# Moving the last step of a strip's recurrence from ahead of the next strip's last weight tile to behind the next strip's convolution, in a hybrid decoder layer

## Chip, cores and metric

One Trainium2 chip, one core. The metric is the device time of one launch in microseconds (us), lower is better; several runs of a kernel are compared by their median.

## What is computed

One inference step of one decoder layer, for 256 prompt tokens and 8 x 8 sample tokens together (320 tokens), model width 2048. The input projection feeds three token mixers (RG-LRU, gated DeltaNet, causal pooling); their gated outputs are summed, projected and added to the residual; a squared-ReLU MLP follows. The part that matters here is the RG-LRU, cut from the reference:

```python
xl, gl, q, k, v, z, b_raw, a_raw, u_pool, g_lru, g_dn, g_pool = split_cols(xn @ w_in)
xl, new_lru_buf = causal_dwconv(xl, lru_buf, lru_conv_w, lru_conv_b)      # 4 taps over time
h, h_last = rg_lru(xl, w_a, b_a, w_x, b_x, lam, h0)
# r, i = sigmoid(xl @ w_a + b_a), sigmoid(xl @ w_x + b_x);  a = exp(-8 r softplus(-lam))
# h[t] = a[t] h[t-1] + sqrt(1 - a[t]^2) (i[t] xl[t])
o_lru = (h * jax.nn.gelu(gl)).astype(x.dtype)
merged = sigmoid(g_lru) * (o_lru @ w_br_lru) + ...
```

## The kernel before

Channels lie on partitions, the 320 tokens on columns. Every weight passes through the kernel once, in tiles of 512 x 256 values (128 x 1024 on chip), through a ring of four slots. SyncE starts the load of a tile into `raw`. ScalarE rounds it to `hi` (`split` in its program, L617), VectorE forms `lo = raw - hi` (`split`, L885), and TensorE multiplies hi and lo parts with the activations' hi and lo parts: 24 matmuls of 320 columns for a tile (`tile`, L1436 to L1438). The four steps are tied by counts:

- SyncE may load tile n+4 when `lo` of tile n is written (`lo_ready`).
- ScalarE may write `hi` of tile n+4 when TensorE is done with tile n (`tile_used`).
- TensorE starts tile n when its `lo` is there, and writes into a PSUM bank when VectorE has emptied it (`evacuated`).

The RG-LRU's 1024 channels are worked on in four strips of 256. A strip has eight weight tiles, 0 to 3 for `xl` and 4 to 7 for `gl`. Strip 0 is written out ahead of a loop; the loop (`Fori(1, 4)`) runs strips 1 to 3 on TensorE, ScalarE and VectorE alike. When `xl` is done, VectorE convolves it in time (`lru_conv`: L885 empties two banks, then L888 and L892, 4 + 12 instructions, into `scratch`), which sets `conv_ready`. TensorE's `gates` waits for it after tile 7 and runs four small products (L1539). Then the next strip's tile 0 begins.

The recurrence of strip `it-1` is worked off during strip `it`, in six steps that stand between the tiles' splits. `walk` (VectorE) places a step with position p behind the split of tile p-1. `walk_ahead` (ScalarE) places it behind the split of tile p, one further on. The order is the same program order as written, engine by engine; nothing reorders it. The steps, by position:

- 3, step 0: the gates' tanh (ScalarE L701, L703), the log of a (VectorE).
- 4, step 1: exp, tanh, square (ScalarE L708 to L710), one VectorE product.
- 5, steps 2 and 3: root (ScalarE L713), the scan (VectorE L1110), and the emptying of the two banks of `gl`.
- 6, step 4: the inner part of GELU (VectorE), its tanh (ScalarE L719).
- 7, step 5: two products on VectorE (L892) form the output; ScalarE rounds it to `o_hi` (L722); VectorE subtracts to `o_lo` (L885) and counts `o_ready`.
- 8: on VectorE `lru_conv` of the strip itself.

Step 5 has a hand-over in both directions: ScalarE waits for `of_ready`, set by VectorE's second product, and VectorE waits for `ohi_ready`, set by ScalarE. Of the four `o_hi`/`o_lo` strips TensorE reads nothing before the next stage (`gated`, L1640 on), whose tile 5 waits for `o_ready` of all four.

The last strip's recurrence (strip 3) is worked off in the first iteration of that next stage, `gated(0, GPL_N, ...)`, with the same positions 3 to 7.

The functions `lru_steps`, `walk`, `walk_ahead`, `lru`, `lru_step`, `conv` and `gates` are those that the text below follows.

Of the kernel before, what the change touches and what calls it, by code (L numbers as in the profile page):

```python
# [46 lines left out]
LRU_N, LRU_T = QKV_N + 6 * 8, QKV_T + 6 * 4  # L47
# [35 lines left out]
def cols(t, index, width, lo=0, n=None, rows=P):  # L83

    n = width if n is None else n
    if isinstance(index, int):
        return t[0:rows, index * width + lo:index * width + lo + n]
    return t[0:rows, bass.ds(index * width + lo, n)]


def build(nc, A):
    with ExitStack() as ctx:
# [455 lines left out]
        def joined(a, b):  # L548

            return {i: [*a.get(i, ()), *b.get(i, ())] for i in {*a, *b}}  # L550

        def walk(split, n0, per, it, tiles, after):

            for j in range(tiles):
                split(n0, per, it, j)
                for step in after.get(j + 1, ()):
                    step()

        def walk_ahead(split, n0, per, it, tiles, after):

            split(n0, per, it, 0)
            for j in range(tiles):
                if j + 1 < tiles:
                    split(n0, per, it, j + 1)
                for step in after.get(j + 1, ()):
                    step()

        def lru_steps(step, it):

            return {pos: [lambda k=k: step(it, k) for k in ks]  # L570
                    for pos, ks in ((3, (0,)), (4, (1,)), (5, (2, 3)), (6, (4,)), (7, (5,)))}

        def qkv_steps(rms, silu, rows):

# [32 lines left out]
        def _(act):  # L607
# [117 lines left out]
            def lru(it, after):  # L725
                walk_ahead(split, LRU_N, 8, it, 8, after)
# [3 lines left out]
                    6: [lambda: row_scalars(3)], 7: [lambda: root(2)]})  # L730
            with act.Fori(1, 4) as it:
                ch.enter(it, 1, LINKS["rglru"])
                lru(it, lru_steps(lru_step, it - 1))
                ch.leave(3, "rglru")

            def gate(it, s, t0, g0):
# [38 lines left out]
            def late(it, t0, h0):  # L775

                steps = {2: [lambda: gate(it, 1, t0, 0)]}
                return steps if h0 is None else joined(steps, dn_steps(dn_step, it + h0, False, True))

            gated(0, GPL_N, GPL_T, 0, lru_steps(lru_step, 3), True)  # L780
            with act.Fori(1, 4) as it:
                gated(it, GPL_N, GPL_T, 0, late(it - 1, GPL_T, 0))
# [95 lines left out]
        def _(dve):  # L878
# [76 lines left out]
            def conv(n0, per, it, j, t, tval, strip, first, ct, bias):  # L955

                tile_done(n0, per, it, j)
                if not first:
                    dve.wait_ge(tail_copied, strip)
                sv = [PAD[m][:, NP + 3:347].rearrange("p (b t) -> p b t", b=DB) for m in range(2)]  # L960
                for m in range(2):
                    scaled(t + m, PAD[m][:, 3:3 + NP], sv[m][:, :, CW - 1:CW - 1 + DT])
                dve.wait_ge(evacuated, tval)
                dve.wait_ge(prefix_ready, strip + 1)
                for w in range(CW):
                    for m in range(2):
                        k = cols(PRM, ct, CW, C_CW + m * CW + w, 1)
                        for src, dst in ((PAD[m][:, w:w + NP], CV[:, m * N:m * N + NP]),
                                         (sv[m][:, :, w:w + DT],
                                          CV[:, m * N + NP:(m + 1) * N].rearrange("p (b t) -> p b t", b=DB))):  # L970
                            if w:
                                ins = stt(dst, src, k, dst, ALU.mult, ALU.add)
                            elif bias is None:
                                ins = ts(dst, src, k, ALU.mult)
                            else:
                                ins = ts(dst, src, k, ALU.mult, bias[m], ALU.add)
                    if w < CW - 1:
                        link(ins)
                ins.then_inc(conv_ready, 1)
# [96 lines left out]
            def lru_conv(it):  # L1076
                conv(LRU_N, 8, it, 3, 0, it * 4 + (LRU_T + 2 + RING), it + 12, False, it * 2 + 24,
                     [cols(PRM, it, 2, C_CB + m, 1) for m in range(2)])
# [47 lines left out]
                    tt(cols(OL, it, 2 * N), GL, cols(OH, it, 2 * N).bitcast(F32), ALU.subtract).then_inc(o_ready, 1)  # L1126

            def lru(it, after):
                walk(split, LRU_N, 8, it, 8, {**after, 8: [lambda: lru_conv(it)]})

            lru(0, {4: [lambda: silu(11)], 6: [lambda: row_scalars(3)], 7: [row_norms]})
            with dve.Fori(1, 4) as it:
                ch.enter(it, 1, LINKS["lru"])
                lru(it, lru_steps(lru_step, it - 1))
                ch.leave(3, "lru")

            def gate(n0, t0, it, s):
# [664 lines left out]
```

## Time and profile before

| | |
|---|---|
| time, median of 3 runs | 2188.42 us (2185.13 to 2188.83) |
| the profiled execution: its own time | 2186.87 us |
| its span, first to last instruction | 2185.1 us |
| TensorE busy | 2149.7 us (98%) |
| VectorE busy | 1222.3 us (56%) |
| ScalarE busy | 784.2 us (36%) |
| GpSimd busy | 175.9 us (8%) |
| mean DMA traffic | 141 GB/s |
| mean granted TensorE clock | 0.994 |
| chain of work that ended last, by engine | TensorE 84%, VectorE 9%, ScalarE 3%, issue 3%, DMA 1% |

The page gives each engine's busy time as a share of the span. TensorE (PE) is busy nearly all the time by its records; the matmuls are pipelined and their ends modelled, so that their starts, not their durations, give the pace. The granted clock is 1.00 at full speed (2.4 GHz) and 0.50 at half (1.2 GHz). The loop over RG-LRU strips 1 to 3 lies between 229 and 325 us of the span.

### The profile page before, as it was taken

The numbers are of one execution on the slowest core, as the hardware profiler recorded it, in microseconds if no ns is written. First come the engines' busy times: TensorE is split into PE (matmuls) and PEld (weight loads), VectorE is DVE, ScalarE is ACT, GpSimd is POOL, SyncE is SP. The second block draws the span as 40 slices with busy tenths as digits, with TensorE's granted clock in tenths as the row PEclk, the third lists the DMA queues.
The fourth block names the chain that finished last, engine by engine and source line by source line (L and its number), as shares of the span: only waits on it lengthen the run. The fifth ranks groups of instructions, "written<-read, shape, count | busy, mean of one in ns | idle before, by whom it ended". The sixth has DMA issues, their size and how long they took to land.

```text
span 2185.1 us, 35787 instructions
## 1 busy us (share of the span) xinstructions
PE 2149.7 (98%) x14515; PEld 2094.4 (96%) x14515; DVE 1222.3 (56%) x1996; ACT 784.2 (36%) x946; POOL 175.9 (8%) x340
## 2 busy tenths in 40 slices
PE   9999998999999999999999999999999999999997
PEld 9998997999998999999999999999999999999997
DVE  7996785555566655555454554444444444444444
ACT  6434553222232222333334343333333333333343
POOL 7000012110022110010000000000000000000001
PEclk9999999999999999999999999999999999999998
DMA  6544443343353433336544444444444444444443
GB/s 218 163 143 128 140 129 121 116 119 116 116 165 106 118 117 116 116 107 212 150 148 155 145 144 152 147 153 146 154 145 154 146 154 146 154 145 154 147 144 106
DMA packets 295609, 308.96 MB, mean 141 GB/s; under 512 B 9712, under 2 KB 290416, under 8 KB 295232
## 3 DMA queue, kind: packets, MB, share of 16 engines
q1 hardware_dynamic: 291616, 291.54, 43.1%
q0 software_dynamic: 3584, 15.55, 2.4%
q8 instruction: 90, 1.47, 0.3%
q14 instruction: 31, 0.25, 0.0%
q10 hardware_dynamic: 288, 0.15, 0.0%
HBM read 298.83 MB, written 8.37 MB: 141 GB/s over the span
## 4 chain that ended last, share of the span: by engine, by line
PE 84%; DVE 9%; ACT 3%; issue 3%; DMA 1%; DVEq 0%; ACTq 0%; SPq 0%
PE main L1436 26%; PE main L1438 25%; PE main L1437 25%; PE aux L1556 6%; DVE scratch L892 2%; DVE lo L885 2%; DVE scratch L885 2%; ACT hi L617 1%; DMA raw<-in_w_in 1%; DVE scratch L889 1%; PE aux L1539 0%; PE aux L1529 0%; DVE scratch L888 0%; DVE merged L885 0%; PE aux L1660 0%
## 5 line engine op out<-in xcount | busy, mean ns | idle before, releaser
L885 DVE TENSOR_TENSOR lo<-raw,hi 128x1024 fp32r<-128x1024 f32 x546 | 667.2, 1230 | 566.6 <-ACT hi L617 560.0
L617 ACT ACTIVATE hi<-raw 128x1024 fp32r<-128x1024 f32 x546 | 573.3, 1056 | 920.6 <-PE main L1438 904.8
L1436 PE MATMUL main<-x_hi,hi 128*128 128x320 f32 x2688 | 842.8, 314 | 2.5 <-DVE x_lo L892 2.0
L1438 PE MATMUL main<-x_hi,lo 128*128 128x320 f32 x2688 | 831.5, 309 | 0.0
L1437 PE MATMUL main<-x_lo,hi 128*128 128x320 f32 x2688 | 831.5, 309 | 0.0
L1436 PEld LDWEIGHTS main<-x_hi,hi 128*128 128x128 f32 x2688 | 505.7, 188 | 10.6 <-issue 5.0
L1437 PEld LDWEIGHTS main<-x_lo,hi 128*128 128x128 f32 x2688 | 505.8, 188 | 0.7
L1438 PEld LDWEIGHTS main<-x_hi,lo 128*128 128x128 f32 x2688 | 505.4, 188 | 0.0
L1436 PE MATMUL main<-o_hi,hi 128*128 128x320 f32 x1408 | 444.6, 316 | 4.6 <-DVE o_lo L885 4.6
L1438 PE MATMUL main<-o_hi,lo 128*128 128x320 f32 x1408 | 435.6, 309 | 0.0
L1437 PE MATMUL main<-o_lo,hi 128*128 128x320 f32 x1408 | 435.5, 309 | 0.0
L1436 PEld LDWEIGHTS main<-o_hi,hi 128*128 128x128 f32 x1408 | 264.8, 188 | 9.2 <-issue 7.1
L1437 PEld LDWEIGHTS main<-o_lo,hi 128*128 128x128 f32 x1408 | 265.0, 188 | 2.0 <-issue 1.9
L1438 PEld LDWEIGHTS main<-o_hi,lo 128*128 128x128 f32 x1408 | 264.9, 188 | 0.0
L1556 PE MATMUL aux<-scratch 128*128 128x128 f32 (+5 forms) x1056 | 155.9, 284 | 6.2 <-DVE scratch L1200 3.2
L1556 PEld LDWEIGHTS aux<-scratch 128*128 128x128 f32 (+1 forms) x1056 | 130.4, 185 | 26.2 <-DVE scratch L885 10.2
L885 DVE TENSOR_TENSOR qkv<-main,qkv 128x320 f32<-128x320 f32 (+1 forms) x144 | 64.0, 486 | 72.9 <-PE main L1438 72.8
L1436 PE MATMUL main<-merged_hi,hi 128*128 128x320 f32 x256 | 79.1, 309 | 0.0
L1437 PE MATMUL main<-merged_lo,hi 128*128 128x320 f32 x256 | 79.1, 309 | 0.0
L1438 PE MATMUL main<-merged_hi,lo 128*128 128x320 f32 x256 | 79.1, 309 | 0.0
L885 DVE TENSOR_TENSOR scratch<-scratch,aux 128x256 f32<-128x256 f32 (+2 forms) x144 | 45.2, 359 | 51.7 <-PE aux L1556 43.6
L544 POOL COPY qkv<-gate 128x640 f32<-128x640 f32 x1 | 0.7, 724 | 867.7 <-ACT gate L854 867.7
(253 smaller groups left out, 1190.8 us busy)
## 6 DMA issues: line engine op xcount, KB each, us to landing
raw<-in_w_in SPq DMA_DIRECT2D x210, 512.0 KB, 3.8
raw<-in_w_up SPq DMA_DIRECT2D x128, 512.0 KB, 3.8
raw<-in_w_down SPq DMA_DIRECT2D x128, 512.0 KB, 3.4
raw<-in_w_back SPq DMA_DIRECT2D x80, 512.0 KB, 3.4
scratch<-in_s_in POOLq DMA_DIRECT2D x8, 512.0 KB, 4.7
out_s_out<-scratch POOLq DMA_DIRECT2D x8, 512.0 KB, 4.6
merged<-in_x SPq DMA_DIRECT2D x8, 320.0 KB, 7.8
qkv<-in_x POOLq DMA_DIRECT2D x1, 2560.0 KB, 10.2
```

The lines of the kernel that those rows point to most:

```text
L544: pool.tensor_copy(acc, GS[:]).then_inc(sq2_used, 1)
L617: act.activation(HI[:, slot * TILE:(slot + 1) * TILE], RAW[:, slot * TILE:(slot + 1) * TILE], ACT.Copy).then_inc(hi_ready, 1)
L885: return dve.tensor_tensor(out, a, b, op)
L889: dve.tensor_scalar(out, a, s1, None, op0)
L892: return dve.scalar_tensor_tensor(out=out, in0=a, scalar=s, in1=b, op0=op0, op1=op1)
L1436: pe.matmul(bank, hi, xh, start=first, stop=False)
L1437: pe.matmul(bank, hi, xl, start=False, stop=False)
L1438: return pe.matmul(bank, lo, xh, start=False, stop=last)
L1556: return pe.matmul(out, a, b, start=True, stop=True)
```

## The change

On VectorE, inside the loop, step 5 of the strip before goes from position 7 to position 8, and `joined` puts it behind the convolution there: the order split 6, step 5, split 7, convolution becomes split 6, split 7, convolution, step 5. On ScalarE the same `last=8` names another position, but `walk_ahead` has no split between positions 7 and 8: its order stays split 7, step 5, next strip's split 0. The steps of strip 3, in the stage after the loop, keep position 7.

```diff
-        def lru_steps(step, it):
+        def lru_steps(step, it, last=7):
 
             return {pos: [lambda k=k: step(it, k) for k in ks]
-                    for pos, ks in ((3, (0,)), (4, (1,)), (5, (2, 3)), (6, (4,)), (7, (5,)))}
+                    for pos, ks in ((3, (0,)), (4, (1,)), (5, (2, 3)), (6, (4,)), (last, (5,)))}
...
             with act.Fori(1, 4) as it:
                 ch.enter(it, 1, LINKS["rglru"])
-                lru(it, lru_steps(lru_step, it - 1))
+                lru(it, lru_steps(lru_step, it - 1, 8))
...
             def lru(it, after):
-                walk(split, LRU_N, 8, it, 8, {**after, 8: [lambda: lru_conv(it)]})
+                walk(split, LRU_N, 8, it, 8, joined({8: [lambda: lru_conv(it)]}, after))
...
             with dve.Fori(1, 4) as it:
                 ch.enter(it, 1, LINKS["lru"])
-                lru(it, lru_steps(lru_step, it - 1))
+                lru(it, lru_steps(lru_step, it - 1, 8))
```

## Rows read from the trace of the kernel before

**Rows 1.** Waits of TensorE between 225 and 425 us: total, times, longest.
```profile
PE main L1436 <- DVE o_lo L885: 4.6, 1, 4.6
PE aux L1539 <- DVE scratch L892: 4.0, 3, 1.3
```

**Rows 2.** Timeline of TensorE around the gates: start, duration, instruction [idle before].
```profile
260.71 0.55 PE L1436 MATMUL main<-x_hi,hi 128*128 128x320 f32 x1
...
288.96 0.31 PE L1438 MATMUL main<-x_hi,lo 128*128 128x320 f32 x1
290.58 2.42 PE L1539 MATMUL aux<-scratch 128*128 128x320 f32 x8 [1.31 <-DVE scratch L892]
292.59 0.55 PE L1436 MATMUL main<-x_hi,hi 128*128 128x320 f32 x1
```

**Rows 3.** Timeline of VectorE, strip 2 of the loop, end.
```profile
277.62 1.22 DVE L885 TENSOR_TENSOR lo<-raw,hi 128x1024 fp32r<-128x1024 f32 x1
279.07 1.68 DVE L892 SCALAR_TENSOR_TENSOR scratch<-scratch 128x640 f32<-128x640 f32 x2 [0.23 <-ACT scratch L719]
281.78 0.83 DVE L885 TENSOR_TENSOR o_lo<-scratch,o_hi 128x640 f32 x1 [1.03 <-ACT o_hi L722]
282.52 1.22 DVE L885 TENSOR_TENSOR lo<-raw,hi 128x1024 fp32r<-128x1024 f32 x1
283.66 1.01 DVE L885 TENSOR_TENSOR scratch<-main,rms_scale 128x256 f32<-128x256 f32 x4
...
286.42 4.11 DVE L892 SCALAR_TENSOR_TENSOR scratch<-scratch,params 128x256 f32<-128x256 f32 x12 [0.16 <-DVE scratch L888]
290.44 3.49 DVE L885 TENSOR_TENSOR lo<-raw,hi 128x1024 fp32r<-128x1024 f32 x3
```

**Rows 4.** Timeline of ScalarE, strip 2 of the loop; the last two rows: strip 3.
```profile
264.66 1.06 ACT L617 ACTIVATE hi<-raw 128x1024 fp32r<-128x1024 f32 x1 [1.60 <-PE main L1438]
...
268.18 1.06 ACT L617 ACTIVATE hi<-raw 128x1024 fp32r<-128x1024 f32 x1 [0.44 <-PE main L1438]
...
278.94 1.05 ACT L617 ACTIVATE hi<-raw 128x1024 fp32r<-128x1024 f32 x1
280.88 0.74 ACT L722 ACTIVATE o_hi<-scratch 128x640 f32 x1 [0.89 <-DVE scratch L892]
281.64 1.28 ACT L617 ACT_TABLE_LOAD   x1
282.93 2.01 ACT L617 ACTIVATE hi<-raw 128x1024 fp32r<-128x1024 f32 x2
...
312.76 0.74 ACT L722 ACTIVATE o_hi<-scratch 128x640 f32 x1 [0.89 <-DVE scratch L892]
313.41 2.00 ACT L617 ACTIVATE hi<-raw 128x1024 fp32r<-128x1024 f32 x2
```

**Rows 5.** Timeline of ScalarE: first step of strip 3's recurrence, behind the loop.
```profile
324.93 0.53 ACT L701 ACTIVATE scratch<-aux,params 128x320 f32<-128x320 f32 x1 [6.14 <-PE aux L1539]
```

**Rows 6.** SyncE's load started after the next strip's first `lo`: time to landing.
```profile
L242 SPq DMA_DIRECT2D raw<-in_w_in x1: 373/373/373, 259.9 to 259.9; - x1
DMA to landing us min/median/max: 3.7/3.7/3.7
...
DMA to landing us min/median/max: 4.8/4.8/4.8
```

**Rows 7.** Timeline of TensorE: starts after waits of four lengths.
```profile
9.04 0.39 PE L1436 MATMUL main<-x_hi,hi 128*128 128x320 f32 x1 [1.99 <-DVE x_lo L892]
...
347.08 0.61 PE L1436 MATMUL main<-o_hi,hi 128*128 128x320 f32 x1 [4.59 <-DVE o_lo L885]
347.48 0.47 PE L1437 MATMUL main<-o_lo,hi 128*128 128x320 f32 x1
347.75 0.47 PE L1438 MATMUL main<-o_hi,lo 128*128 128x320 f32 x1
...
359.93 0.44 PE L1582 MATMUL aux<-ident,scratch 128*128 128x128 f32 x2 [2.14 <-DVE scratch L885]
...
685.65 0.69 PE L1582 MATMUL aux<-ident,scratch 128*128 128x128 f32 x2 [2.86 <-DVE scratch L885]
```

**Rows 8.** Windows: length, busy by engine (PE, PEld, DVE, ACT, POOL), PEclk, DMA share, GB/s.
```profile
5.00:10.00 5.00, 3.01 (x23) 2.85 (x23) 3.15 (x8) 3.96 (x7) 4.27 (x26) 1.00 1.07 376
10.00:20.00 10.00, 10.00 (x71) 10.00 (x70) 6.09 (x8) 6.55 (x11) 8.06 (x8) 1.00 1.06 373
255.00:265.00 10.00, 8.67 (x53) 7.77 (x52) 8.52 (x19) 3.18 (x6) 0.00 (x0) 1.00 0.39 111
360.00:364.00 4.00, 4.00 (x17) 3.42 (x18) 0.72 (x3) 0.78 (x3) 0.00 (x0) 0.57 0.02 4
684.80:691.70 6.90, 6.05 (x23) 5.26 (x24) 1.85 (x8) 1.47 (x4) 0.00 (x0) 0.51 0.00 0
```

## Prediction

> **What bounds the kernel now.** I read three views in this order. First the busy shares: TensorE 98%, so only its idle time and its clock can move the end. Then the waits of TensorE in the stretch of the change [rows 1]: three waits of 1.3 us at the gates (L1539), each released by the convolution on VectorE, and one of 4.6 us at tile 5 of the next stage, released by `o_lo` of strip 3. Then the timelines of the three engines over one strip, to see what leads to the convolution's end.
>
> I take strip 2 of the loop as the template and count from the start of its tile 0 on TensorE, 260.71; call that T. The next strip's tile 0 starts at 292.59, T+31.88 [rows 2]. Eight tiles end for issue at T+28.40 (last matmul starts at 288.96, and they follow each other by 0.15), TensorE waits until 290.58, and the gates take 2.01 to the next tile 0. The floor of a strip is thus 28.40 + 2.01 = 30.41, and 1.47 of the 31.88 is the wait (1.31 by the records, whose ends are modelled).
>
> What ends that wait is a loop through all engines. ScalarE's `hi` of tile 4 starts at 264.66, T+3.95, released by TensorE's end of tile 0; `hi` of tile 5 at T+7.47, released by the end of tile 1; `hi` of tile 7 at T+18.23 [rows 4]. VectorE then does step 5 at 279.07, waits 1.03 for `o_hi`, writes `o_lo`, does `lo` of tile 7 at 282.52 and the convolution up to 290.53 [rows 3]. The gates start 0.05 later.
>
> **The change, part by part.** No instruction is added or removed; the same 3 + 1 instructions of step 5 run three times in another place. No DMA is issued by step 5. ScalarE's instruction stream is the same as before. GpSimd isn't passed: its tail copies wait for the two banks emptied by the convolution, which come earlier, and its prefixes for the next convolution are copied long before.
>
> (a) What is taken from ahead of the convolution. `lo` of tile 7 no longer waits for step 5, only for `hi` of tile 7, which ends at 278.94 + 1.05 = 279.99 [rows 4]. It starts at 280.03, T+19.32, in place of 282.52: 2.49 earlier. From there to the convolution's end are 8.01 (282.52 to 290.53) [rows 3], so it ends at T+27.33. TensorE comes to the gates at T+28.40. The wait of 1.47 is gone, with 1.07 to spare. The gates are done at T+30.41.
>
> (b) What is put behind it. VectorE's two products take 1.68 from T+27.25 to T+28.93. ScalarE has stood at step 5 since `hi` of tile 7 ended (T+19.28), as it can't pass its own wait. `o_hi` starts 0.13 after the products (280.75 to 280.88), at T+29.06. **Queued behind that wait on ScalarE are the next strip's `hi` 0 and 1**, which before were done at about T+24.2. At the loop's start stands an activation table load, then `hi` 0: 2.05 after the start of `o_hi` (280.88 to 282.93) [rows 4]. So `hi` 0 runs from T+31.11 to T+32.15. VectorE needs 0.04 and 1.22 for `lo` 0: T+33.41. TensorE starts tile 0 at about T+33.46, not at T+30.41. That is 33.46 - 31.88 = **1.58 later than before**, in place of 1.47 earlier: the wait has moved from before the gates to after them, and grown to 3.05. `o_lo`, 0.83 on VectorE, fits in while ScalarE does its table load and `hi` 0.
>
> (c) How often. Three iterations have the moved step. The first two are followed by the loop's start with its table load: 2 x 1.58 = 3.16. The third is followed by the next stage, where `hi` 0 comes 0.65 after the start of `o_hi` (312.76 to 313.41) [rows 4]: T+29.71. Tile 0 would start at T+32.0 to 32.1, 0.2 late. That stage has a wait of 4.6 at tile 5, but it absorbs nothing, for what ends it is strip 3's recurrence, which starts on ScalarE with L701 at 324.93, T+32.34 in its strip (tile 0 at 292.59) [rows 5]. Ahead of L701 stand `hi` 0, 1, 2. Before, they were done early and L701 waited for the gates. Now they run from T+29.71 at about 1.0 each (2.00 for two), so that L701 starts at T+32.6: 0.25 late, and tile 5 with it. Sum so far: 3.16 + 0.25 = **3.4 us slower**.
>
> (d) The next strip's own loop. `hi` 4 there waits for TensorE's tile 0 (T'+3.95, T' the late start) and for its load, started at 259.94, 0.23 after `lo` 0 ended at 259.71 [rows 6]. With a landing time of 3.7 it is there at T'+3.9 and costs nothing; with 4.8, as once in this trace, `hi` 4 starts at T'+5.0, and 0.44 of that is caught by the wait ahead of `hi` 5 [rows 4], so 0.6 is lost. Bounds: 0 and 0.6 per strip; I take 0, as two of three loads landed in 3.7. The two banks of `gl` are emptied in the same relation to T' as before.
>
> (e) The clock. The wait after the gates isn't harmless in its length. By the records the gates end 0.40 after the next tile could start (290.58 + 2.42 = 293.00 against 292.59), so the idle time of TensorE is 33.46 - 30.41 - 0.40 = 2.65. In this trace waits of 1.31 (255 to 265 us) and of 1.99 (at 9.04) left the granted clock at 1.00, that of 2.14 at 359.93 was followed by half clock (0.57 over 360 to 364), that of 2.86 at 685.65 by 0.51 over 6.9 us, and that of 4.59 by half clock as well [rows 7, 8]. The new wait of 2.65 lies between two that were followed by half clock, not far above one that wasn't. At half clock matmuls start every 0.27 (347.48, 347.75) in place of 0.147, so 3.4 us of it cost 3.4 x (1 - 0.147/0.27) = 1.5. It falls on tiles 0 and 1, whose ends release `hi` 4 and 5, so it delays the whole loop of (a) and (b). Bounds for one such wait: 0 (as after 1.99) and 3.1 (6.9 us at half clock). There are two such waits. I give each 6 in 10 to bring the clock down, and take one of the two: **1.5**. The third wait (T+30.81 to T+32.05, about 1.2) is like those before the gates that did nothing.
>
> The Trainium skill, "TensorE: Matmul & The Clock Gate", section "Why this matters for your kernels", advises only against longer idle gaps between bursts than this one; by it the clock would stay up here and the sum would be 3.4. The waits of 2.14 and 2.86 in this trace speak against it. I keep it as a rival.
>
> The table load costs 1.28 and `hi` 0 starts directly behind it, 2.05 after `o_hi` began [rows 4]. The Trainium skill, "ScalarE: Activation LUTs", section "What ACT_TABLE_LOAD costs", adds a drain of about 1.38 to each switch of tables; by it two loads on the path would cost about 2.8 more, a sum of 7.7 as an estimate from the page. The row shows no such gap between `o_hi` (ends 281.62), the load and `hi` 0, so I go by the row.
>
> **Sum.** 3.16 + 0.25 + 1.5 = 4.9. The span becomes 2185.1 + 4.9 = 2190.0, the profiled execution's own time 2186.87 + 4.9 = 2191.8. That execution lies 1.55 below the median of the runs; on the median I predict 2188.42 + 4.9 = **2193.3 us**. The runs shown spread over 3.7 us, so I call under 0.2% (4.4 us) no difference.
>
> **The rivals.**
>
> *No fall of the clock* (0.17). Only the moved wait counts: +3.4, 2191.8. For it: the wait of 1.99 left the clock alone. Against: those of 2.14 and 2.86 didn't.
>
> *Both waits bring it down* (0.28): +6.4, 2194.8; if one of the stretches is as long as the one at 685 us, +8.0.
>
> *Faster: the hold on ScalarE is hidden* (0.05). If `hi` 0 of the next strip were worked off before ScalarE stands at `of_ready`, the three waits at the gates would go and nothing come back: -1.47 x 3 = -4.4, 2184.0. It decides at tile 0's `lo`: ready before T+30.41 it is a gain, and my chain has it at T+33.41. For it speaks that ScalarE is idle for 9.8 us while it stands there and the slots are free; against it the program order, in which step 5 comes first.
>
> *The table load costs more when nothing hides it* (0.05): if VectorE's `lo` 0 finds `hi` 0 later than 2.05 after `o_hi` by another 1.4, twice, the sum is 7.7, 2196.1. Against it stands the row of the same load behind the same `o_hi`.
>
> **How the numbers follow.** My forecast, one fall, gets 0.42; the rest, 0.03, is for what I don't see. The low end: no fall, 2191.8, less some 2 for the runs' spread and for the half-clock stretches elsewhere, which may come out shorter: 2189.5. The high end: two falls with a longer stretch, 2196.4, and a late load in each strip, 1.2: 2197.5. Faster: the hidden hold and a little for the spread, 0.07. The case without a fall lies mostly within 0.2%, the forecast is 0.22% and so about 4 in 10 within, two falls hardly: 0.31 for the same. Slower: 0.62.
>
> **What the profile after would show.** Right: no wait of L1539 for L892; two new waits of about 3 us of L1436 (tile 0) for `lo` L885, and one near 1.2; `o_hi` (L722) about 8 us later in the strip, after an idle time of about 9.8 on ScalarE; strips 33.5 us or more apart, and half clock for some us after at least one of the new waits; the wait of 4.6 at tile 5 unchanged. Wrong: `hi` 0 of the next strip ahead of `o_hi`, or the convolution still ending after TensorE's tile 7, or a wait at tile 5 that shrinks by what came before it.

## The result

| | before | changed |
|---|---|---|
| median of 20 runs | 2186.55 us (2182.57 to 2188.83) | 2192.27 us (2190.01 to 2194.83) |
| ratio to before | | 1.0028, 95% interval 1.0022 to 1.0035 |
| profiled execution: span | 2185.1 us | 2193.1 us |
| mean granted clock there | 0.994 | 0.992 |

The changed kernel is slower by 5.7 us on the medians, by 4.8 to 7.7 us on the interval. I had forecast 4.9 more, 2193.3 us against a median before of 2188.42 from three runs; with twenty runs that median is 1.9 lower. So the time itself is only 1.0 off because two misses cancel in part: the base was 1.9 too high and the added time 0.8 too low. The profiled execution of the changed kernel is the slowest of its twenty runs (2194.83), so its trace shows more than the median's loss: 8.0 in place of 5.7.

The two largest groups of TensorE's waits between 225 and 425 us of the changed kernel (who waited, for whom, total, times, longest), to be read against [rows 1]:

```profile
PE main L1436 <- DVE lo L885: 6.9, 3, 2.8
PE main L1436 <- DVE o_lo L885: 4.8, 1, 4.8
```

The three waits of L1539 for the convolution are gone. In their place L1436, tile 0 of the next strip, waits three times for its `lo`. The timeline of TensorE shows where, against [rows 2]: the gates of strips 1, 2 and 3 start at once, and tile 0 behind them is late.

```profile
257.31 2.31 PE L1539 MATMUL aux<-scratch 128*128 128x320 f32 x8
262.44 0.63 PE L1436 MATMUL main<-x_hi,hi 128*128 128x320 f32 x1 [2.82 <-DVE lo L885]
262.87 0.47 PE L1437 MATMUL main<-x_lo,hi 128*128 128x320 f32 x1
263.13 0.47 PE L1438 MATMUL main<-x_hi,lo 128*128 128x320 f32 x1
...
293.46 2.31 PE L1539 MATMUL aux<-scratch 128*128 128x320 f32 x8
298.57 0.41 PE L1436 MATMUL main<-x_hi,hi 128*128 128x320 f32 x1 [2.80 <-DVE lo L885]
...
328.37 2.31 PE L1539 MATMUL aux<-scratch 128*128 128x320 f32 x8
331.99 0.41 PE L1436 MATMUL main<-x_hi,hi 128*128 128x320 f32 x1 [1.31 <-DVE lo L885]
...
354.61 0.60 PE L1436 MATMUL main<-o_hi,hi 128*128 128x320 f32 x1 [4.76 <-DVE o_lo L885]
```

ScalarE's timeline over strip 2's end, against [rows 4]: 9.74 us of idle time in front of `o_hi`, then the table load, then four `hi` in one go.

```profile
283.29 1.04 ACT L617 ACTIVATE hi<-raw 128x1024 fp32r<-128x1024 f32 x1
294.08 0.74 ACT L722 ACTIVATE o_hi<-scratch 128x640 f32 x1 [9.74 <-DVE scratch L892]
294.83 1.28 ACT L617 ACT_TABLE_LOAD   x1
296.13 3.90 ACT L617 ACTIVATE hi<-raw 128x1024 fp32r<-128x1024 f32 x4
```

And VectorE's, against [rows 3]: the last tile's `lo` waits for its `hi`, the convolution follows (L892, x12, up to 292.37), then the two products; the next strip's `lo` waits for ScalarE.

```profile
284.37 1.23 DVE L885 TENSOR_TENSOR lo<-raw,hi 128x1024 fp32r<-128x1024 f32 x1 [1.17 <-ACT hi L617]
...
288.26 4.11 DVE L892 SCALAR_TENSOR_TENSOR scratch<-scratch,params 128x256 f32<-128x256 f32 x12 [0.15 <-DVE scratch L888]
292.28 1.68 DVE L892 SCALAR_TENSOR_TENSOR scratch<-scratch 128x640 f32<-128x640 f32 x2
294.98 0.82 DVE L885 TENSOR_TENSOR o_lo<-scratch,o_hi 128x640 f32 x1 [1.03 <-ACT o_hi L722]
297.22 3.50 DVE L885 TENSOR_TENSOR lo<-raw,hi 128x1024 fp32r<-128x1024 f32 x3 [1.41 <-ACT hi L617]
```

The windows around the end of the first new wait and behind the second (length, busy time by engine, granted clock, DMA) show the clock, against [rows 8]:

```profile
261.00:268.00 7.00, 5.56 (x21) 5.57 (x22) 5.77 (x7) 4.55 (x8) 0.00 (x0) 0.55 0.62 180
...
299.00:303.00 4.00, 4.00 (x19) 4.00 (x19) 2.85 (x5) 2.69 (x6) 0.00 (x0) 0.57 0.74 198
```

Tile 5 of the next stage starts at 354.61, before at 347.08 [rows 7]: 7.5 of the 8.0 by which this profiled execution is longer are there before the stage's tile 5.

### The profile page after: what moved, and what is told of

The parts are those of the page before. It is cut to its first block, busy times and chain, and to the rows that moved or that the text cites. A ratio compares the mean times of both kernels' runs of the same rounds, so it can differ in the third digit from the quotient of the medians.

```text
span 2193.1 us, 35787 instructions
## 1 busy us (share of the span) xinstructions
PE 2154.9 (98%) x14515; PEld 2099.5 (96%) x14515; DVE 1221.5 (56%) x1996; ACT 783.3 (36%) x946; POOL 174.9 (8%) x340
## 4 chain that ended last, share of the span: by engine, by line
PE 84%; DVE 9%; ACT 3%; issue 3%; DMA 1%; DVEq 0%; ACTq 0%; SPq 0%
PE main L1436 26%; PE main L1438 25%; PE main L1437 25%; PE aux L1556 6%; DVE scratch L892 2%; DVE lo L885 2%; DVE scratch L885 2%; ACT hi L617 2%; DMA raw<-in_w_in 1%; DVE scratch L889 1%; PE aux L1529 0%; DVE merged L885 0%; DVE scratch L888 0%; PE aux L1660 0%; DVE qkv L892 0%
## 5 line engine op out<-in xcount | busy, mean ns | idle before, releaser
L1436 PE MATMUL main<-x_hi,hi 128*128 128x320 f32 x2688 | 844.2, 314 | 9.2 <-DVE lo L885 7.4
L1436 PEld LDWEIGHTS main<-x_hi,hi 128*128 128x128 f32 x2688 | 507.3, 189 | 18.5 <-issue 11.7
L1436 PE MATMUL main<-o_hi,hi 128*128 128x320 f32 x1408 | 445.3, 316 | 4.8 <-DVE o_lo L885 4.8
L1436 PEld LDWEIGHTS main<-o_hi,hi 128*128 128x128 f32 x1408 | 265.4, 188 | 9.5 <-issue 7.4
L1436 PE MATMUL main<-merged_hi,hi 128*128 128x320 f32 x256 | 79.1, 309 | 0.0
L885 DVE TENSOR_TENSOR o_lo<-scratch,o_hi 128x640 fp32r<-128x640 f32 (+1 forms) x44 | 36.3, 825 | 60.7 <-ACT o_hi L845 50.4
```

The lines of the kernel that those rows point to most:

```text
L885: return dve.tensor_tensor(out, a, b, op)
L1436: pe.matmul(bank, hi, xh, start=first, stop=False)
```

## The experiments

Each of the eight kernels was timed beside the kernel before. The table gives the ratio with its 95% interval, and what it is in us of 2187. The last column is the distance from one strip's gates to the next strip's in the profiled execution (from the first L1539 of one to the first of the other), strips 0 to 1, 1 to 2, 2 to 3: the pace of the loop, of which eight tiles and the gates alone take 30.4.

| kernel | median, us | ratio (95%) | in us | gates to gates, us |
|---|---|---|---|---|
| before | | 1 | | 31.81, 31.89, 31.89 |
| change | 2192.27 | 1.0028 (1.0022 to 1.0035) | +6.1 | 30.32, 36.15, 34.91 |
| e1 products ahead, `o_lo` behind | 2182.24 | 0.9978 (0.9969 to 0.9987) | -4.8 | 30.32, 30.31, 30.30 |
| e2 e1 with ScalarE's hold | 2187.94 | 1.0002 (0.9993 to 1.0011) | +0.4 | 30.32, 32.46, 33.99 |
| e3 change, wait filled | 2190.27 | 1.0016 (1.0007 to 1.0025) | +3.5 | 30.31, 33.41, 33.40 |
| e4 change, ScalarE's loop written out | 2186.90 | 1.0001 (0.9992 to 1.0010) | +0.2 | 30.38, 31.96, 31.92 |
| e5 before, ScalarE's loop written out | 2185.23 | 0.9999 (0.9990 to 1.0008) | -0.2 | 31.77, 31.87, 31.86 |
| e6 step 5 between split and convolution | 2192.77 | 1.0032 (1.0021 to 1.0044) | +7.0 | 32.76, 32.82, 34.43 |
| e7 e1 and strip 3's tail closed up | 2178.47 | 0.9967 (0.9955 to 0.9979) | -7.2 | 30.32, 30.32, 30.30 |
| e8 e6, wait filled | 2188.89 | 1.0011 (1.0002 to 1.0020) | +2.4 | 32.75, 32.84, 32.83 |

**e1: only the wait for `o_hi` and the subtraction go behind the convolution.** Step 5 on VectorE is cut in two: the two products, which release ScalarE, stay where they were before the change. The last strip's step 5, in the stage behind the loop, keeps its order. The edit is against the kernel before.

```diff
-                else:
+                elif k == 5:
                     dve.wait_ge(gth_ready, it + 1)
                     link(stt(GL, G2, 1.0, GL, ALU.add, ALU.mult))
                     dve.wait_ge(h_ready, it + 1)
                     stt(GL, TR, 0.5, GL, ALU.mult, ALU.mult).then_inc(of_ready, 1)
+                else:
                     dve.wait_ge(ohi_ready, it + 1)
...
-                walk(split, LRU_N, 8, it, 8, {**after, 8: [lambda: lru_conv(it)]})
+                walk(split, LRU_N, 8, it, 8, joined({8: [lambda: lru_conv(it)]}, after))
...
-                lru(it, lru_steps(lru_step, it - 1))
+                lru(it, joined(lru_steps(lru_step, it - 1), {8: [lambda: lru_step(it - 1, 6)]}))
```

> Only the last of step 5's instructions, the subtraction to o_lo with its wait for o_hi, goes behind the convolution; the two products stay ahead of the last tile's split, so ScalarE is released as early as before. My theory (the loss comes from ScalarE standing in front of the next strip's first tile): the convolution still starts 1.8 us earlier, ends 0.4 us ahead of TensorE's tile 7, and hi of tile 0 is not held, so the three waits of 1.47 us go and nothing comes back: 4.4 us faster than before. Rival one (it is the wait for o_hi and the o_lo subtraction behind the convolution that make the next lo late): slower by about 1 us a strip. Rival two (the convolution does not set the strip's pace): no change.

It is 4.8 us faster than before. The timelines of ScalarE, VectorE and TensorE over strip 2's end (line numbers have moved by one on TensorE):

```profile
279.15 0.74 ACT L722 ACTIVATE o_hi<-scratch 128x640 f32 x1 [0.89 <-DVE scratch L892]
279.91 1.28 ACT L617 ACT_TABLE_LOAD   x1
281.20 2.01 ACT L617 ACTIVATE hi<-raw 128x1024 fp32r<-128x1024 f32 x2
```
```profile
277.35 1.68 DVE L892 SCALAR_TENSOR_TENSOR scratch<-scratch 128x640 f32<-128x640 f32 x2 [0.23 <-ACT scratch L719]
278.95 1.22 DVE L885 TENSOR_TENSOR lo<-raw,hi 128x1024 fp32r<-128x1024 f32 x1
...
282.82 4.11 DVE L892 SCALAR_TENSOR_TENSOR scratch<-scratch,params 128x256 f32<-128x256 f32 x12 [0.15 <-DVE scratch L888]
286.85 0.82 DVE L885 TENSOR_TENSOR o_lo<-scratch,o_hi 128x640 f32 x1
287.58 3.49 DVE L885 TENSOR_TENSOR lo<-raw,hi 128x1024 fp32r<-128x1024 f32 x3
```
```profile
287.38 2.32 PE L1540 MATMUL aux<-scratch 128*128 128x320 f32 x8
289.29 0.55 PE L1437 MATMUL main<-x_hi,hi 128*128 128x320 f32 x1
```

VectorE loses neither the 1.03 in front of `o_lo` nor a wait for `hi` 7, the convolution is done at 286.93, 0.45 before TensorE wants it, and ScalarE has the next strip's `hi` 0 and 1 done by 283.2. No wait of TensorE is left in the loop, and ScalarE isn't held at step 5 in front of the next strip's tiles. Both rivals fall: the `o_lo` subtraction behind the convolution costs nothing, and the convolution did set the pace.

**e2: the hold alone is put back.** ScalarE is made to stand at step 5 until the convolution is done; VectorE's order stays e1's.

```diff
                     act.wait_ge(of_ready, it + 1)
+                    if not isinstance(it, int):
+                        act.wait_ge(conv_ready, it + 14)
```

> The kernel of e1, in which ScalarE alone is made to wait for the end of the convolution before it rounds to o_hi; VectorE's order is e1's. My theory: hi 0 of the next strip comes 2.05 us after o_hi, which starts at T+28.1, tile 0 starts at T+32.5 in place of T+31.88: 0.6 us a strip slower than before in the first two, strip 3's recurrence about 0.6 us earlier than before behind the third; in sum 0.6 us slower than before and 5 us slower than e1, idle time of TensorE at tile 0 about 1.7 us, clock not touched. Rival (the place of VectorE's work, not ScalarE's hold, makes the loss): as e1, 4.4 us faster.

It is level with before (+0.4), 5.2 us slower than e1, as expected. The profile adds what the expectation had wrong: the third distance is 33.99. TensorE's second new wait, of 1.86, was followed by half clock, shown here by its timeline and the window behind it (line numbers moved by two and three):

```profile
293.53 0.41 PE L1439 MATMUL main<-x_hi,hi 128*128 128x320 f32 x1 [1.86 <-DVE lo L887]
```
```profile
294.50:298.00 3.50, 3.50 (x16) 3.50 (x15) 2.34 (x5) 2.16 (x5) 0.00 (x0) 0.51 0.94 263
```

The first, of 1.87, wasn't. VectorE's order is the same in e1 and e2, so the gain of e1 is lost by ScalarE standing in front of the next strip's tiles, with the half clock that follows one of the waits it makes.

**e3: the changed kernel with the new wait filled by idle products.** They compute nothing that is used.

```diff
+            def fill(it):
+                pe.wait_ge(evacuated, it * 4 + (LRU_T + 5))
+                for i in range(5):
+                    pe.matmul(MB[0][:, 0:N], ones[:], R[:], start=True, stop=True)
...
-                lru(it, {7: [(7, lambda: gates(it))]})
+                lru(it, {7: [(7, lambda: gates(it)), (7, lambda: fill(it))]})
```

> The changed kernel with five idle products (ones times rms_scale, 320 columns, overwritten by the next tile) on TensorE behind the gates, about 2.5 us that end before tile 0's lo is there. They compute nothing that is used. My theory: the moved wait alone costs 3.4 us, the rest of the 5.7 us measured for the change is half clock after the two idle stretches; with the stretches filled the clock stays at 1.00 there and the kernel is 3.4 us slower than before, with a best run no better than the changed kernel's best. Rival (the wait itself costs all, the clock nothing): 5.7 us slower as the change.

3.5 us slower than before (1.5 to 5.5), where the plain change is 6.1 by its ratio (4.8 to 7.7). The rows of TensorE around the gates of strip 1 (each idle product shows as two instructions):

```profile
256.74 2.32 PE L1539 MATMUL aux<-scratch 128*128 128x320 f32 x8
258.90 2.85 PE L1552 MATMUL main<-rms_scale,ones 128*128 128x320 f32 x10
261.88 0.41 PE L1436 MATMUL main<-x_hi,hi 128*128 128x320 f32 x1
```

Tile 0 comes no earlier than its `lo`, and the distances are 33.41 and 33.40, where the plain change has 36.15 and 34.91. The window over the loop has the clock at 1.00:

```profile
225.00:335.00 110.00, 109.75 (x695) 104.16 (x694) 83.67 (x157) 61.17 (x76) 8.87 (x33) 1.00 0.47 139
```

My expectation of the best run was wrong: the best of this kernel, 2187.91, is below the changed kernel's best, 2190.01. The granted clock of each run, a mean over the whole kernel, fits that: it is at most 0.994 in the changed kernel's 20 runs, and 0.995 or more in five of e3's 11. The means over the runs are 0.9927 and 0.9942, with 0.9940 in the 33 runs of the kernel before beside e3. Where in those runs the half clock fell is not on record.

**e4 and e5: ScalarE's loop written out,** in the changed kernel and, as a control, in the one before.

```diff
-            with act.Fori(1, 4) as it:
-                ch.enter(it, 1, LINKS["rglru"])
-                lru(it, lru_steps(lru_step, it - 1, 8))
-                ch.leave(3, "rglru")
+            for it in range(1, 4):
+                lru(it, lru_steps(lru_step, it - 1, 8))
```

> The changed kernel with ScalarE's loop over strips 1 to 3 written out, so that the table load at the loop's start is not needed. My theory: hi 0 comes 0.65 us after the start of o_hi in place of 2.05, tile 0 starts at T+32.05, the wait on TensorE is 1.2 us and does not bring the clock down: 0.17 us twice and 0.25 us once, 0.6 us slower than before. Rival (the hand-over for o_hi itself is the price, not the load): 3 us slower or more.

> The kernel before with ScalarE's loop over strips 1 to 3 written out and the table load at its start gone. Control for e4. My theory: before the change the load stands where ScalarE has time (hi 0 and 1 are done 4 us before they are needed), so its loss changes nothing: within 0.5 us of before. Rival (the load costs there too): 1.3 us a strip faster.

e4 is level with before (+0.2, -1.7 to +2.2). ScalarE's timeline at the end of strip 2:

```profile
289.48 0.74 ACT L722 ACTIVATE o_hi<-scratch 128x640 fp32r<-128x640 f32 x1 [9.65 <-DVE scratch L890]
290.12 3.88 ACT L617 ACTIVATE hi<-raw 128x1024 fp32r<-128x1024 f32 x4
```

Without the load `hi` 0 comes 0.64 after the start of `o_hi`, and TensorE's waits at tile 0 are 1.30, 1.28 and 1.21, after which the clock stayed at 1.00 in the loop. e5 is unchanged (-0.2, -2.2 to +1.8), and so are its distances: the same load ahead of time costs nothing. The load is thus part of the moved wait only because the hold puts it on the path. The hold itself, with its hand-over, costs what the change gains at the gates: 31.96 and 31.92 against 31.89.

**e6: step 5 behind the last split, but ahead of the convolution.**

```diff
-                walk(split, LRU_N, 8, it, 8, joined({8: [lambda: lru_conv(it)]}, after))
+                walk(split, LRU_N, 8, it, 8, joined(after, {8: [lambda: lru_conv(it)]}))
```

> Step 5 goes behind the last tile's split but stays ahead of the convolution: split 6, split 7, step 5, convolution. My theory: the convolution ends 1.0 us later than before (VectorE waits 1.2 us for hi 7, then again 1 us for o_hi), ScalarE is released 2.1 us later, which is harmless; the wait at the gates grows from 1.47 to 2.45 us: 2.9 us slower, and up to 3 us more where the clock falls. No wait at tile 0. Rival (any order that does the last split early gains): 1 us a strip faster.

7.0 us slower (4.6 to 9.6), above the upper end of 5.9 but with an interval that holds it. The distances 32.76 and 32.82 are the 0.9 to 1.0 a strip that the order gives; the third, 34.43, has half clock in it. TensorE's rows at the gates show it, with the gates of strip 2 stretched to 4.00:

```profile
259.38 2.42 PE L1539 MATMUL aux<-scratch 128*128 128x320 f32 x8 [2.28 <-DVE scratch L892]
292.20 4.00 PE L1539 MATMUL aux<-scratch 128*128 128x320 f32 x8 [2.25 <-DVE scratch L892]
326.63 2.42 PE L1539 MATMUL aux<-scratch 128*128 128x320 f32 x8 [2.26 <-DVE scratch L892]
```

Three waits of the same length, and only one of them was followed by half clock before the next stage's tile 5.

**e8: e6 with the wait filled,** four idle products ahead of the gates.

```diff
-                lru(it, {7: [(7, lambda: gates(it))]})
+                lru(it, {7: [(7, lambda: fill(it)), (7, lambda: gates(it))]})
```

> e6 (step 5 between the last split and the convolution), with four idle products on TensorE, about 2.0 us, ahead of the gates in the stretch in which it waits. They compute nothing that is used. e6 came out 7.0 us slower where its order gives 2.9 (0.98 a strip). If the rest is half clock after waits of 2.3 us, it is now about 3 us slower than before and the granted clock stays 1.00 through the loop. Rival (e6's order costs more than the wait at the gates shows): 7 us slower as e6.

+2.4 (0.4 to 4.4), with even distances of 32.75, 32.84 and 32.83. That is the price of e6's order alone. The rest of its 7.0 goes with the clock: its mean over the runs is 0.9920 in e6 and 0.9942 in e8. Of that only the one stretch in the loop is placed by the profile, 34.43 - 32.83 = 1.6; the profiled execution of e6 also has a lower clock around tile 5 of the next stage than e8's, 0.77 and 0.89 over 345 to 375, though that tile waits 4.59 in both. Why is open.

**e7: e1, and the steps of strip 3's recurrence closed up** in the stage behind the loop. The first lines are ScalarE's, the last VectorE's.

```diff
+            tail = {pos: [lambda k=k: lru_step(3, k) for k in ks]
+                    for pos, ks in ((3, (0, 1)), (4, (2,)), (5, (3, 4)), (6, (5,)))}
-            gated(0, GPL_N, GPL_T, 0, lru_steps(lru_step, 3), True)
+            gated(0, GPL_N, GPL_T, 0, tail, True)
...
+            tail = {pos: [lambda k=k: lru_step(3, k) for k in ks]
+                    for pos, ks in ((3, (0, 1)), (4, (2,)), (5, (3, 4, 5)), (6, (6,)))}
```

> e1, and in the stage behind the loop the steps of strip 3's recurrence stand closer: steps 0 and 1 together behind tile 2, steps 3 and 4 (and VectorE's products of step 5) together behind tile 4, the rest one tile earlier. If the wait of 4.6 us at tile 5 is the length of strip 3's chain with two splits of each engine standing in it, o_lo is ready about 2.7 us earlier, the wait falls to about 1.9 us and less half clock follows: 2.7 to 4 us faster than e1, 7.5 to 9 us faster than before. Rival (the splits moved back make a lo late and TensorE waits at tile 4 or 5 for it): no gain over e1, a wait of main for lo in place of that for o_lo.

2178.5 us, 7.2 us faster than before (4.6 to 9.8), just short of the 7.5 to 9 expected, with the lowest median of these kernels. TensorE's rows with a wait between 336 and 344 us:

```profile
339.06 0.39 PE L1441 MATMUL main<-o_hi,hi 128*128 128x320 f32 x1 [1.72 <-DVE o_lo L887]
343.19 0.85 PE L1561 MATMUL aux<-head_rows,row_pickers 48*128 48x320 f32 x4 [2.13 <-POOL head_rows L452]
```

The wait at tile 5 is 1.72 in place of e1's 4.60, and tile 5 starts 21.6 after strip 3's gates in place of 24.5, so the 2.7 that was expected there came. No wait for a `lo` took its place. Part of it came back: a new wait of 2.13 for GpSimd's `head_rows`, which was not in the prediction for this kernel. GpSimd waits in its program for `o_lo` of strip 3 before it forms those rows, and TensorE now reaches them sooner: after 2.0 of work from tile 5's start, at full clock, where e1 took 3.5, at half clock. The gain over e1 is 3.8 us on the medians and 2.4 by the ratios, whose intervals overlap.

## Why the prediction was right

**The gates' wait goes (a): right.** It was to end 1.07 before TensorE's need. In the changed kernel the gates follow tile 7 without a wait in all three strips, and strip 0's gates to strip 1's are 30.32 (floor 30.41 as I had it).

**The wait moves behind the gates and grows (b): right.** I had 33.46 from tile 0 to tile 0; e3's trace, undisturbed by the clock, gives 33.41 from gates to gates. `o_hi` after an idle time of 9.8 on ScalarE: 9.75 and 9.74. `hi` 0 behind `o_hi` by 2.05: 296.13 - 294.08 = 2.05. TensorE's idle time 2.65: 2.82 and 2.80. With the two products back in their old place, so that ScalarE isn't held, the loss turns into 4.8 of gain (e1); the hold put back alone, 0.9 shorter than in the change (ScalarE idle for 8.80 in front of `o_hi`), takes 5.2 away again (e2).

**2 x 1.58 + 0.25 = 3.4 for the moved wait (c): right for the two strips, too high for the third.** e3 measures 3.5, within 1.5 to 5.5. Its trace is sharper: from strip 0's gates to tile 5 of the next stage it takes 123.36 where the kernel before takes 120.20, 3.16 more, and 3.13 of that is there when strip 3 begins. Tile 5's wait absorbed nothing, as I had it (4.76 after 4.59 in the change), but the 0.25 isn't there: L701 of strip 3's recurrence starts 32.38 after that strip's tile 0 in e3's trace, and 32.34 after it in the kernel before. (TensorE's wait at tile 5 is 3.64 in e3, as the idle products keep it busy longer there than the wait of 1.31 they replace; tile 5 comes 26.24 after strip 3's gates in e3 and in the change alike.) The rows of e3's trace, strip 0's gates, strip 3's tile 0, L701 and tile 5:

```profile
226.43 2.32 PE L1539 MATMUL aux<-scratch 128*128 128x320 f32 x8
...
295.27 0.41 PE L1436 MATMUL main<-x_hi,hi 128*128 128x320 f32 x1
...
327.65 0.51 ACT L701 ACTIVATE scratch<-aux,params 128x320 f32<-128x320 f32 x1
...
349.79 0.39 PE L1436 MATMUL main<-o_hi,hi 128*128 128x320 f32 x1 [3.64 <-DVE o_lo L885]
```

**The late load (d)** played no part: `hi` 4 of the next strip waited for TensorE in all three strips of the changed kernel's trace.

**The clock (e): right as a mechanism, probably low in size.** Both waits brought the clock down in the profiled execution, the second as I sized it: TensorE lost 34.91 - 33.41 = 1.5. The first brought 6.8 us of half clock (0.80 over 258 to 275) and cost 36.15 - 33.41 = 2.7. Over many runs the change's ratio less e3's is about 2.6 us; my term was 1.5. The granted clocks give a second figure: 0.9942 - 0.9927 = 0.0015 of 2190 us is 3.3 us of full clock lost, that is 6.6 us more at half clock, worth 3.0 us by the price I used, as an estimate. Neither is sharp: the intervals of the two ratios are 1.5 to 2 us to either side, and a term of 1.5 is not excluded. That the sum came within 0.8 of the result is helped a little by the 0.25 too much in (c).

**The rivals.** The hold was not hidden. The table load cost 1.4 a strip (e4 against the change in the distance from `o_hi` to `hi` 0: 2.05 - 0.64), less than the 2.66 that the Trainium skill, "ScalarE: Activation LUTs", section "What ACT_TABLE_LOAD costs", gives for a switch with its drain; in the changed kernel it stands on the path and `hi` 0 follows directly behind its 1.28. And the idle gaps of 2.8, which the Trainium skill, "TensorE: Matmul & The Clock Gate", section "Why this matters for your kernels", counts as short enough, were followed by half clock here, as were one of 1.86 in e2 and one of 2.25 in e6.

## What to carry to other kernels

A step that hands work to another engine and back is two steps. Move the part that waits for the answer, and leave the part that the other engine waits for where it is: e1 differs from the change in nothing else and is 10 us faster on the medians. (Part of that is clock: without its half clock the change would cost about 3.5, as e3.) Before moving a wait on one engine, write down what stands behind it in program order on the engine at its other end. And an idle stretch of TensorE of some 1.9 us or more may cost more than itself in this kernel, for half clock can follow it.

## What was not expected

- Waits of the same length differ in what follows. Of e6's three waits of 2.25 to 2.28 one was followed by half clock in the loop, and of e2's two of 1.87 and 1.86 the second. What decides it no run here shows. In the kernel before none of the three of 1.3 was, nor of e4's three of 1.2 to 1.3, nor the change's third of 1.31.
- Idle products that keep TensorE busy while it waits pay for themselves: e3 is 2.6 us faster than the change by the ratios (their intervals just overlap), and e8 4.6 us faster than e6 (they don't), though neither does any useful work more.
- The table load at the start of ScalarE's loop is there because of the loop: written out, it is gone (e4, e5).
- The wait at tile 5 of the next stage is nearly the same in the traces of before and after (4.59 and 4.76), but the granted clock behind it isn't: it is 0.77 over 345 to 375 in the changed kernel's trace and 0.89 over 338 to 368 in that of the kernel before, each from some 9 us ahead of tile 5. By tile 5 that execution was 7.5 behind, at its end 8.0.
